# Last layer's queries and keys ahead of its values, with token rows turned across all tokens, and five smaller moves, in a three-layer float32 kernel

## The reference

```python
def first_block(...):
    for i in range(DEPTH):                       # 0: convolution and state space, 1: gated linear attention
        m = even_mixer(h, ...) if i % 2 == 0 else odd_mixer(h, ...)
        h = layer_norm(DEEPNORM_ALPHA * h + m, ln_g[i, 0], ln_b[i, 0])
        h = layer_norm(DEEPNORM_ALPHA * h + memory_cross_attention(h, mem, ...), ln_g[i, 1], ln_b[i, 1])
        h = layer_norm(DEEPNORM_ALPHA * h + sq_relu_mlp(h, mlp_w1[i], mlp_w2[i]), ln_g[i, 2], ln_b[i, 2])

def second_block(x, ...):
    h = rms_norm_2(x, norm_gain[l], RMS_EPS)
    proj = jnp.einsum('bsd,de->bse', h, w_in[l])
    (qa, ka, va, ga, qb, kb, vb, gb, qc, kc, vc, fc, gc, gm) = jnp.split(proj, offsets, axis=-1)
    ya = diff_attention(...)           # 4 heads of two maps
    yb = sliding_window_attention(...) # window of 128
    yc = forgetting_attention(...)
    merged = gates[:, :, 0] * ua + gates[:, :, 1] * ub + gates[:, :, 2] * uc
    return rms_norm_2(x + jnp.einsum('bsd,de->bse', merged, w_o[l]), final_gain, RMS_EPS)
```

## Time and profile before

| | us |
|---|---|
| median of 3 runs (lowest, highest) | 2294.74 (2294.55, 2296.74) |
| the profiled execution, its own time | 2293.56 |
| its span | 2291.7 |
| PE busy | 2238.5 |
| DVE busy | 1273.0 |
| ACT busy | 924.2 |
| POOL busy | 164.4 |

### The profile page before, as it was taken

How to read it: one execution, slowest core, us unless ns; L and a number is a source line. 1 busy time by engine, 2 the same in 40 slices (tenths; PEclk the granted TensorE clock), 3 DMA queues, 4 the chain that set the end, 5 groups by cost and what they waited for, 6 DMA issues and landing times.

```text
span 2291.7 us, 27734 instructions
## 1 busy us (share of the span) xinstructions
PE 2238.5 (98%) x11201; PEld 1841.4 (80%) x11201; DVE 1273.0 (56%) x1886; ACT 924.2 (40%) x1690; POOL 164.4 (7%) x149
## 2 busy tenths in 40 slices
PE   8999999999999999999999999999989999999998
PEld 6886888878788888888887788888867688887777
DVE  5999887745733434735574573333452843642664
ACT  3253764343422323345434232232253534533453
POOL 1110000210400000400022040000000000000000
PEclk9999999999999999999999999999999999999999
DMA  5352245323333232321152223323233132123113
GB/s 172 104 156 74 74 133 193 116 92 128 104 111 95 97 103 92 121 74 56 62 187 84 66 93 112 109 92 92 92 115 106 37 92 74 56 92 92 55 38 119
DMA packets 181588, 226.95 MB, mean 99 GB/s; under 512 B 17587, under 2 KB 140214, under 8 KB 180438
## 3 DMA queue, kind: packets, MB, share of 16 engines
q1 hardware_dynamic: 169686, 192.23, 26.6%
q10 hardware_dynamic: 9664, 22.33, 2.8%
q0 software_dynamic: 2112, 10.64, 1.4%
HBM read 213.78 MB, written 9.18 MB: 97 GB/s over the span
## 4 chain that ended last, share of the span: by engine, by line
PE 88%; DVE 7%; ACT 3%; issue 1%; DMA 0%; ACTq 0%; DVEq 0%; SPq 0%
PE gemm L657 26%; PE gemm L659 26%; PE gemm L658 26%; PE aux L790 2%; DVE w_lo L2323 1%; PE aux L1047 1%; PE aux L1069 1%; DVE x_lo L2346 1%; DVE work L2461 1%; PE aux L1425 1%; PE gemm L966 1%; ACT w_hi L1480 1%; PE aux L1411 1%; DVE mxs L3037 1%; PE aux L1380 1%
## 5 line engine op out<-in xcount | busy, mean ns | idle before, releaser
L657 PE MATMUL gemm<-x_hi,w_hi 128*128 128x512 f32 x1288 | 515.9, 401 | 12.3 <-DVE x_lo L2346 6.4
L658 PE MATMUL gemm<-x_lo,w_hi 128*128 128x512 f32 x1288 | 503.1, 391 | 0.0
L659 PE MATMUL gemm<-x_hi,w_lo 128*128 128x512 f32 x1288 | 503.1, 391 | 0.0
L2323 DVE TENSOR_TENSOR w_lo<-raw,w_hi 128x1024 fp32r<-128x1024 f32 x222 | 284.2, 1304 | 270.6 <-ACT w_hi L1480 269.7
L1480 ACT ACTIVATE w_hi<-raw 128x1024 fp32r<-128x1024 f32 x222 | 228.1, 1053 | 271.2 <-PE gemm L659 246.8
L657 PE MATMUL gemm<-w_hi,y_hi 128*128 128x512 f32 (+1 forms) x832 | 321.6, 386 | 1.3 <-DVE h L2410 1.3
L658 PE MATMUL gemm<-w_lo,y_hi 128*128 128x512 f32 (+1 forms) x832 | 317.0, 381 | 0.0
L657 PEld LDWEIGHTS gemm<-x_hi,w_hi 128*128 128x128 f32 x1288 | 242.8, 189 | 82.7 <-issue 18.2
L2319 DVE TENSOR_TENSOR w_lo<-raw,w_hi 128x1024 fp32r<-128x1024 f32 x140 | 168.2, 1221 | 252.8 <-ACT w_hi L1478 243.6
L659 PE MATMUL gemm<-w_hi,y_lo 128*128 128x512 f32 x768 | 298.9, 389 | 0.0
L659 PEld LDWEIGHTS gemm<-x_hi,w_lo 128*128 128x128 f32 x1288 | 242.6, 188 | 51.6
(11 more groups left out here) (345 smaller groups left out, 2817.1 us busy)
## 6 DMA issues: line engine op xcount, KB each, us to landing
raw<-in_mlp_w_dram SPq DMA_DIRECT2D x64, 1024.0 KB, 5.4
raw<-in_w_in_dram SPq DMA_DIRECT2D x31, 1024.0 KB, 5.2
raw<-in_odd_w_in_dram SPq DMA_DIRECT2D x12, 1024.0 KB, 5.3
raw<-in_even_w_in_dram SPq DMA_DIRECT2D x10, 1024.0 KB, 5.2
raw<-in_even_w_in_dram SPq DMA_DIRECT2D x16, 512.0 KB, 5.2
raw<-in_xa_w_k_dram SPq DMA_DIRECT2D x8, 1024.0 KB, 5.2
raw<-in_xa_w_v_dram SPq DMA_DIRECT2D x8, 1024.0 KB, 5.2
raw<-in_even_w_out_dram SPq DMA_DIRECT2D x8, 1024.0 KB, 5.1
```

The source lines that it names most:

```text
L657: pe.matmul(dst, a_hi, b_hi, start=first, stop=False)
L658: pe.matmul(dst, a_hi, b_lo, start=False, stop=False)
L659: return pe.matmul(dst, a_lo, b_hi, start=False, stop=last)
L2323: dve.tensor_tensor(w_lo[:, s % W_SLOTS, :, :], raw[:, s // 2 % RAW_SLOTS, :, half], w_hi[:, s % W_SLOTS, :, :].bitcast(F32), ALU.subtract)\
```

## The change

1. **Passage of the last layer.** `qk_a` comes ahead of `v_a` in the plan. XN is turned by `turn_rows` (four columns across all tokens), the other four columns are turned between the matmuls (`row_fill`), and the operands are written a column of 512 tokens at a time. The values are computed by `gemm_rows` after the queries and keys.
2. **Start.** The first panel's two halves are loaded one after the other, the second after all of x and the first half have landed; ACT and DVE split only the first piece ahead of the last tile of x.
3. **Waits.** Ahead of each branch's units PE waits for the last chunk of the values (in b of `kv_b`), not of the gate.
4. **POOL.** In the norms a0 and a1 `full_rows` also waits until the third chunk of the MLP behind it has been copied out.
5. **Gate work.** In branch a ACT's `gate_rows` stands ahead of the exponentials. Inside the units PE stops at step 60 of 64, after them at 62, and does the last two behind the turns of the output; ACT takes the last gate chunk out after the operands of the up projection.
6. **Small.** The low-rank gate rows of layer 1 (`glow`) are computed ahead of the last panel of queries and keys; in the last norm the tile before the last is scaled in one 1024-wide DVE instruction.

```diff
-            if b == "a":
-                rows("v_a", "w_in_2", 0, base[b] + D, 1)
             add(f"qk_{b}", "w_in_2", 0, range(base[b], base[b] + D, PANEL), FM)
-            if b == "c":
-                rows("v_c", "w_in_2", 0, base[b] + D, 1)
+            rows(f"v_{b}", "w_in_2", 0, base[b] + D, 1)
...
-            load(0)
+            load_first(0)
             for t in range(TT):
                 sp.wait_ge(x_loaded[t], 16)
+            sp.wait_ge(raw_loaded[0], 16)
+            load_first(1)
             load(1)
...
                 wait_aux(pool, ("turn", name, KC - 1))
+                if name in ("a0", "a1"):
+                    chunk_read(pool, stage_chunk("mlp" + name[1]) + 2)
...
-            gemm("gla_qk", x_hi, x_lo, wide="chunks", **row_fill("f0", h))
+            gemm("gla_qk", x_hi, x_lo, panels=3, wide="chunks", **row_fill("f0", h))
             small_rows("glow", 1, 16)
+            gemm("gla_qk", x_hi, x_lo, panels=1)
...
-                    gate_products(b, gate_steps(b, n, len(us)))
+                    gate_products(b, min(gate_steps(b, n, len(us)), KC * KC - 4))
...
-                gate_products(b, KC * KC)
-                at["gate"] = 0
-                at["panel"] += 4
+                gate_products(b, KC * KC - 2)
...
                     ins.then_inc(aux_done, 1)
+                gate_products(b, KC * KC)
+                at["gate"] = 0
+                at["panel"] += 4
                 gemm(f"up_{b}", y_hi, y_lo, ready=lambda k: aux_read(pe, name, k))
...
-            values_by_tokens("v_a")
-            gemm("qk_a", x_hi, x_lo)
+            turn_rows("rms", XN)
+            gemm("qk_a", x_hi, x_lo, wide="chunks", **row_fill("rms", XN))
+            gemm_rows("v_a", x_hi, x_lo, halves=1)
             gemm_rows("g_a", x_hi, x_lo, halves=1)
-            chunk_read(pe, stage_end_chunk("g_a") - 1)
+            chunk_read(pe, stage_end_chunk("v_a") - 1)
...
                     if t == TT - 1 and i == 0:
-                        split_to(0)
+                        split_chunk()
...
                 if t == TT - 2:
                     split_chunk()
-                    token_operand(0)
-                if t == TT - 1:
-                    split_chunk()
-                    token_operand(1)
...
-            token_operand(2)
-            token_operand(3)
+            for k in range(KC):
+                column("rms", k)
+                if k in (3, 4):
+                    split_chunk()
...
+                    if b == "a":
+                        gate_rows(gate_steps(b, n, len(us)) // KC)
                     if n + AHEAD[b] < len(us):
                         exps(us[n + AHEAD[b]])
-                    gate_rows(gate_steps(b, n, len(us)) // KC)
+                    if b != "a":
+                        gate_rows(min(gate_steps(b, n, len(us)) // KC, KC - 1))
...
-                        act.wait_ge(S["out_rstd"], t + 1)
-                        act.wait_ge(S["gained"], t + 1)
-                        act.activation(OUT[:, t, 0:512], OUT[:, t, 0:512], ACT.Identity, scale=rstd[:, 0, t:t + 1])\
-                           .then_inc(S["out_first"], 1)
+                        if t != TT - 2:
+                            act.wait_ge(S["out_rstd"], t + 1)
+                            act.wait_ge(S["gained"], t + 1)
+                            act.activation(OUT[:, t, 0:512], OUT[:, t, 0:512], ACT.Identity,
+                                           scale=rstd[:, 0, t:t + 1]).then_inc(S["out_first"], 1)
...
                 if t == TT:
+                    split_chunk()
                     dve.wait_ge(S["rms_rstd"], TT)
                     dve.tensor_scalar(XN[:, t - 1, :], h[:, t - 1, :], rstd[:, 1, t - 1:t], None, ALU.mult)\
                        .then_inc(row_xn, 1)
-                    token_rest(2)
-                    token_rest(3)
```

More of the change, by code:

```diff
@@ L196, in aux_plan @@
     e += ln("m1") + attention(1) + ln("a1")
-    e += [("turn", "rms", t, i) for t in range(TT) for i in range(2)]
+    e += ln("rms")
     e += units("A", [(hd, t) for hd in range(4) for t in range(TT)], 2, 1, True) + [("At", j) for j in range(4)]
@@ L820, in column_ready @@
             def column_ready(name, k):
-                pe.wait_ge(x_ready, KC * ROW_NORMS.index(name) + k + 1)
+                if name == "rms":
+                    aux_read(pe, "turn", name, k)
+                else:
+                    pe.wait_ge(x_ready, KC * ROW_NORMS.index(name) + k + 1)
             def row_fill(name, src):
@@ L1570, in column @@
             def column(name, k):
-                aux_read(act, "turn", name, k)
-                act.activation(x_hi[:, k, :], XF[k % 2], ACT.Copy).then_inc(x_hi_done, 1)
+                if name == "rms":
+                    bank = wait_aux(act, ("turn", name, k))
+                    operand_hi(x_hi[:, k, :], bank[:, :], x_hi_done, par_col("norm_gain_2", k))
+                else:
+                    aux_read(act, "turn", name, k)
+                    act.activation(x_hi[:, k, :], XF[k % 2], ACT.Copy).then_inc(x_hi_done, 1)
             def layer_norm(name):
@@ L2110, in _ @@
             mlp(1)
-            def token_operand(t):
-                tok = slice(t * P, (t + 1) * P)
-                for i in range(2):
-                    bank = wait_aux(act, ("turn", "rms", t, i))
-                    for k in range(4):
-                        operand_hi(x_hi[:, 4 * i + k, tok], bank[:, k * P:(k + 1) * P], x_hi_done,
-                                   par_col("norm_gain_2", 4 * i + k))
             logs()
@@ L3002, in _ @@
                 B = b.upper()
-                for stage in (f"qk_{b}", f"kv_{b}", "" if b == "a" else f"v_{b}", f"g_{b}"):
+                for stage in (f"qk_{b}", f"kv_{b}", f"v_{b}", f"g_{b}"):
                     if stage == "g_c":
```

103 lines of the change are left out of this document (31 added, 72 removed).

## The result

The changed kernel's median is 2280.86 us (2280.75 to 2283.5, four runs) against 2294.81 (2294.55 to 2296.74, four runs): ratio 0.994, 95% interval 0.9923 to 0.9957, 13.95 us faster. The forecast was 2286.5, with 2281.5 as its lower end; the direction was right, the gain 1.7 times as large as the 8.3 forecast, and the time 0.6 outside the range. In a second comparison the same pair stood at 2281.74 and 2296.11.

What follows compares the result with a forecast made beforehand. PE, busy 98% of the span, was taken as the bound, with its idle and half-clock time to win. Terms -2.1 - 3.7 - 0.7 + 1.6 - 2.0 - 0.8 - 0.6 = -8.3 gave 2286.5 us, range 2281.5 to 2292.0.

Steps and rivals of the forecast that it cites:

- start: Kernel start: first matmul near 14.7 instead of 16.77, as a wait and one split go: -2.1 us.
- POOL's passes: Both MLPs: with POOL started behind the third chunk, PE's waits for w_lo and x_lo go: -3.7 us.
- low-rank rows: Layer 1's low-rank gate rows, computed earlier: PE's wait at L1115 for ACT's copy goes: -0.7 us.
- b: Branch b: earlier start of units and held gate steps covering waits ahead of the up projection: -0.75 us.
- the passage: Last layer's passage: one gap of 11.6 us replaces several waits, 15.1 against 13.3 before: +1.6 us.
- the tail: Kernel end: L2300 of the tile before the last leaves ACT's path ahead of the last square: -0.6 us.
- Branch c: Branch c: start wait goes, held steps gain 0.3, last values lose cover for ACT's copy: -0.25 us.
- Units of a: Branch a's units: half the waits for ACT's copy and half a chance of the half-clock stretch, -2.0 us; start and hold +0.2.
- Rival 1: Branch a's units keep none of their waits and clock stretches vanish in c too: -13.3, so 2281.4 us; chance 0.12.
- Rival 2: POOL's contention only changes place, w_lo waits return, passage gets a second half-clock stretch: 2291.8 us; chance 0.18.
- Rival 3: The passage's 11.6 us gap leaves the clock at half far beyond one stretch; with nine further, 2301.8 us; chance 0.05.
- the sign of one half-clock window behind the gap: Last layer's passage: one gap of 11 to 12 us should be followed by one half-clock window, priced 1.7 us.

Runs made afterwards that it cites:

- Experiments 6 and 7: Changed kernel with PE again waiting for the gate's last chunk ahead of units: in all branches, c 3.9 us longer; in c alone, c 2.53 longer, median 2285.10.
- experiment 8: Changed kernel with the held gate steps given back, all 64 ahead of the output's turns: median 0.3 us lower.
- experiment 4: Changed kernel with ACT's gate_rows in branch a behind the exponentials again: units of a 3.12 us longer, median 3.5 higher.
- experiment 9: Changed kernel with 31 matmuls without use in PE's idle time of the last layer's passage: that stage 1.8 to 2.0 us shorter.
- experiments 1 and 2: Kernel before with only POOL's passes moved late: 5.2 us below before; changed kernel with only those passes put back: 6 to 7 us above changed kernel.

## Why the forecast was wrong

The direction and most mechanisms were right: start, POOL's passes, low-rank rows, b, and the passage as a small loss each came out within 1 us of their terms. Five things were mis-sized, all in one direction but the tail. Behind the first two stands the clock: the prediction reads it at half "in two stretches of 3.4 us", but before's trace has four ahead of its end, one behind the first product and one at the start of c's units:

```profile
2126.10:2129.50 3.40, 3.40 (x13) 2.46 (x12) 3.33 (x5) 0.00 (x0) 0.00 (x0) 0.50 0.09 12
```

1. **Branch c, -0.25 forecast, -1.99 measured.** The step that failed: "c likewise, though its next wait comes at once". The forecast counted the wait and not the clock behind it. Before's stretch at the start of c's units was taken into rival 1 only. Experiments 6 and 7 put wait and stretch back by this one line, for 3.9 and 2.5. The sum by the runs is 0.95 for the wait and 1.5 for the stretch, less 0.6 for the held steps (experiment 8), 1.87, and 0.12 behind the up projection's start. That the stretch stayed away in both profiles of the changed kernel is likely by the change (without the wait it came in two of ten), not certain.
2. **Units of a, -1.8 forecast with its start, -2.79 measured.** "I take half of the waits and half a chance of the stretch": the order of ACT is worth 3.1 (experiment 4), 1.4 of waits and the whole stretch, less 0.3 for the held steps (experiment 8). Half a chance for a stretch that directly follows a wait of 2.0 was the wrong price.
3. **POOL's passes, -3.7 forecast, -4.67 measured.** The mechanism held, the unit was wrong. A wait in the list is worth more than its figure. In the earlier trace rows the wait is 0.48, but from the start of the matmul before it to the start of the one behind it are 0.87 instead of 0.23, and the one behind takes 0.50 instead of 0.40: matmuls overlap by 0.16 when they run on, and the first after a wait starts anew. That is 0.3 more for each of three waits: 3.7 + 0.9 = 4.6.
4. **The passage, +1.6 forecast, +0.9 to +1.1 measured.** At 0.2267 from one large matmul to the next, the 384 of the stage are 87.0, so the passage itself took 14.4 before and 15.3 after. The forecast's 15.1 is near the second, though its gap came out a microsecond longer than forecast and its half-clock stretch was 10.2 us long, not 3.4; the stretch cost far less than half of that, as PE was idle in much of it (experiment 9). Before's side of the sum, 13.3, was the one too small: it lacks the wait of 0.8 for w_lo at L2319, and the 0.3 behind waits of point 3.
5. **The tail, -0.6 forecast, -0.34 measured** with the end of w_o. The 0.72 went, and the last transfer queued behind the one before it.

Terms 1 to 4 together are 1.7 + 1.0 + 1.0 + 0.6 = 4.3 too little gain, the tail 0.3 too much: 8.3 + 4.0 = 12.3, less 0.5 by which the start and b fell short there, against 11.7 in the second profile of the changed kernel. What is left to 13.95 is mostly the step that the median lies 1.2 above the profiled execution, kept as a constant. It isn't one: for the changed kernel the median lay 2.6 below the profiled execution in the first comparison and at it in the second. Before's executions range from 2293.8 (mean clock 0.996) to 2300.0 (0.993), and its profile, 2293.56, happened to be the fastest of all; the changed kernel's three shortest of the first comparison have 0.997. The change also took away places where the clock fell, which may have brought the median nearer to the best execution; no run shows that by itself. The range had its own slip: with the unit term at its bound of -5.9 the sum gives 2282.5, not the 2281.5 that was written.

Rival 1 (2281.4) had nearly the right sum by partly the right places: a's stretch and c's both went. It asked for all of a's waits, of which 1.6 stayed, and had none of the 1.0 more of the MLPs or the change of the median's distance, so its number is partly luck. Rival 2 is refuted by experiments 1 and 2. Rival 3 didn't happen: 13.7 us was the longest stretch in any profile here. But its argument against, that each window ends after 3.4 us, was wrong, and so was the sign of one half-clock window behind the gap: the stretch began within the gap and ran for 10.2. How far the stretch in a1's passage depends on the change stays open, and so does why two profiles with the narrow wait had c's.

## What to carry to other kernels

Where the matrix engine is the bound, price a wait with what follows it: 0.3 us for the matmuls' new start, and a half-clock stretch where the trace shows one right behind it, as here behind a wait of 2.0 in branch a and behind one of 0.69 and 2.2 us of matmuls eight columns wide in c; remove such waits first, even if the wait itself is cheap. Price the stretch by PE's busy time in it, of which it cost a third to a half here, not by its length. Contention between two engines needs no cure where a store of finished work covers it: move it there. And when one profile of each kernel is compared, first list the half-clock stretches of both, since some go by execution.

## What the hardware showed that was not expected

- The granted clock fell for 3.4, 6.8, 10.2 or 13.7 us at a time, and where it did differed between executions of one program: at the start in one profile of the changed kernel and not in the other, in a1's passage for 6.8 and not at all.
- With 31 large matmuls without use in the waits of the last passage (PE busy 10.23 of 12.00) the clock was at 2.4 GHz throughout, and with 36 too; in all eight profiles of the same passage without them it stood at 1.2 GHz for 10.2 or 13.7 us. The 31 gave back 1.8 to 2.0 us.
- A wait listed as 0.69 cost 0.95, and one listed as 0.48 about 0.75: the first matmul behind it takes 0.50 instead of 0.40.
- DVE beside POOL: y_lo 1665 ns for 693, y_hi 1515, w_lo 1762 to 2312 for 1222. The Trainium skill ("SBUF — State Buffer", "Who interferes with whom") says that the later of two such instructions blocks until the first is done; the durations fit that in both places of POOL's passes, though they don't show which of the two blocked. The prediction puts the slowing down to instructions that read two operands; y_hi, which reads one, is slowed as well, from 426 (604 to 700 us in before) to 1515.
